# Ends of layers computed in two halves of 256 tokens in a fused four-layer kernel

## What is computed

```python
# layers 0 and 1
h = x * (1 + scale) + shift                  # modulated input of the layer
y = mixer(h)                                 # ends in  mix @ w_out
x = layer_norm(ALPHA * x + (1 + gate) * y, ln_g[l], ln_b[l])
# layers 2 and 3
h = rms_norm(x, norm_g) * (1 + scale) + shift
x = x + gate * (mixer(h) @ w_out)
# end
return rms_norm(x, final_g)
```

## Time and profile before

| | us |
|---|---|
| median of 3 runs | 1336.09 |
| lowest and highest run | 1335.06 and 1337.81 |
| the profiled execution | 1338.26 |
| its span in the profile | 1336.1 |
| PE busy, share of the span | 1300.1, 97% |
| DVE, ACT, POOL busy | 933.7, 573.0, 358.1 |
| mean granted clock of PE, as a share of full speed | 0.992 |

### The profile page before, as it was taken

The page is one execution under the profiler, slowest core; times in us unless marked ns, Lnnn a source line. Parts: engine busy times, 40 slices in busy tenths (PEclk is TensorE's granted clock), DMA queues, the critical chain, the costliest instruction groups (busy, mean ns, idle before and its releaser), DMA issues.

```text
span 1336.1 us, 17324 instructions
## 1 busy us (share of the span) xinstructions
PE 1300.1 (97%) x6589; PEld 1099.5 (82%) x6589; DVE 933.7 (70%) x1347; ACT 573.0 (43%) x863; POOL 358.1 (27%) x257
## 2 busy tenths in 40 slices
PE   6999999999999999999999999999999999999997
PEld 5998888778778888888888788888888788888885
DVE  7765655786667558888678788776784577776663
ACT  1422322221154347666422387653352477634440
POOL 1200200055520004655434122122115322321123
PEclk9999999999989999999999899999999999999998
DMA  9566566456445520111343212214433112211111
GB/s 379 172 207 185 183 201 189 133 154 194 155 119 160 158 87 20 41 52 49 95 141 112 111 64 71 87 48 138 130 99 118 51 64 67 91 64 64 64 63 63
DMA packets 33938, 155.14 MB, mean 116 GB/s; under 512 B 6720, under 2 KB 6848, under 8 KB 22592
## 3 DMA queue, kind: packets, MB, share of 16 engines
q1 hardware_dynamic: 33856, 154.04, 35.9%
HBM read 151.92 MB, written 2.10 MB: 115 GB/s over the span
## 4 chain that ended last, share of the span: by engine, by line
PE 83%; DVE 7%; issue 4%; ACT 3%; POOL 1%; DMA 1%; SPq 0%; DVEq 0%; POOLq 0%; ACTq 0%
PE bank L881 24%; PE bank L883 23%; PE bank L882 23%; PE bank L1204 2%; PE bank L1189 1%; PE bank L1208 1%; PE bank L1049 1%; DVE keep L2272 1%; DVE acc L1769 1%; ACT w_hi L1424 1%; PE bank L888 1%; POOL beta L2395 1%; PE bank L1177 1%; DMA ada_first<-adat 1%; PE bank L1176 1%
## 5 line engine op out<-in xcount | busy, mean ns | idle before, releaser
L881 PE MATMUL bank<-h_lo,w_hi 128*128 128x512 f32 (+1 forms) x1014 | 398.0, 392 | 6.9 <-DVE h_lo L1918 2.5
L883 PE MATMUL bank<-h_hi,w_hi 128*128 128x512 f32 (+1 forms) x1014 | 393.7, 388 | 0.0
L882 PE MATMUL bank<-h_hi,w_lo 128*128 128x512 f32 (+1 forms) x1014 | 393.4, 388 | 0.0
L1727 DVE TENSOR_TENSOR w_lo<-w_raw,w_hi 128x2048 fp32r<-128x2048 f32 (+2 forms) x91 | 206.8, 2272 | 74.6 <-ACT w_hi L1424 74.4
L881 PEld LDWEIGHTS bank<-h_lo,w_hi 128*128 128x128 f32 x1014 | 190.5, 188 | 47.9 <-issue 5.5
L883 PEld LDWEIGHTS bank<-h_hi,w_hi 128*128 128x128 f32 x1014 | 190.3, 188 | 39.6
L882 PEld LDWEIGHTS bank<-h_hi,w_lo 128*128 128x128 f32 x1014 | 190.5, 188 | 38.0 <-issue 0.2
L1424 ACT ACTIVATE w_hi<-w_raw 128x2048 fp32r<-128x2048 f32 (+2 forms) x91 | 166.7, 1832 | 92.9 <-PE bank L883 86.2
L1769 DVE SCALAR_TENSOR_TENSOR acc<-ada_raw,cond_four,acc 128x1024 f32<-128x1024 f32 x62 | 87.9, 1418 | 3.8 <-DMA ada_raw<-adat 0.8
L1506 ACT ACTIVATE tmp<-bank 128x512 f32<-128x512 f32 x48 | 28.8, 600 | 115.6 <-PE bank L883 114.4
L2395 POOL TENSOR_TENSOR beta<-beta,mats 128x256 f32<-128x256 f32 (+1 forms) x40 | 43.8, 1117 | 63.5 <-ACT beta L1686 63.5
(11 more groups left out here) (370 smaller groups left out, 2609.6 us busy)
## 6 DMA issues: line engine op xcount, KB each, us to landing
w_raw<-wt SPq DMA_DIRECT2D x83, 1024.0 KB, 5.4
ada_raw<-adat SPq DMA_DIRECT2D x256, 128.0 KB, 2.9
ada_first<-adat SPq DMA_DIRECT2D x16, 512.0 KB, 12.1
ada_raw<-adat SPq DMA_DIRECT2D x32, 256.0 KB, 5.7
w_raw<-wt SPq DMA_DIRECT2D x8, 640.0 KB, 4.0
spare_raw<-wt SPq DMA_DIRECT2D x3, 1024.0 KB, 7.1
x<-xt SPq DMA_DIRECT2D x4, 512.0 KB, 15.6
out<-outf SPq DMA_DIRECT2D x8, 256.0 KB, 2.2
```

The costliest lines, as they stand in the source:

```text
L881: pe.matmul(dst, ah, bl, start=start, stop=False, skip_group_check=True)
L882: pe.matmul(dst, al, bh, start=False, stop=False, skip_group_check=True)
L883: return pe.matmul(dst, ah, bh, start=False, stop=stop, skip_group_check=True)
L1727: dve.tensor_tensor(w_lo[wb[T]][:, 0:n], w_raw[wb[T]][:, 0:n], f(w_hi[wb[T]][:, 0:n]), ALU.subtract).then_inc(w_lo_done, 1)
```

## The change

A new function `border` writes the steps between two layers. The last chunk (layers 2 and 3: the last two) is computed for tokens 0 to 255 first, then for 256 to 511 in another bank. Between portions of the right half's products stand the left half's sums, its root and its broadcast. Then come the next layer's four chunks for the left half of block 0, the right half's sums, and further items; an item is a block of features for a group of tokens: blocks 0 to 3 left (items 0 to 3), blocks 0 to 3 right (4 to 7), blocks 4 to 7 whole (8 to 11). All dummy matmuls behind the statistics go. Every operation on the way (residual add, square, root, norm, hi, full value, lo, final scaling, output DMA) is done per half for blocks 0 to 3 and the last chunk; POOL's sum for the next to last chunk in layers 2 and 3 is done per half too.

Beside that: the spare tile of each layer is now the first of the two instead of the second, so it is loaded and split one step earlier; one ada piece moves from tile 27's step to tile 31's; the gain sums begin at product 10 of the left half instead of product 8 of the whole; clearing `q_low` moves behind the last item of layer 2; the streams of layer 1 (`x` times `ln_g` plus `ln_b` on ACT) move behind items 8 to 11, two per item.

```diff
--- before.py
+++ after.py
...
+HALF_BLOCKS = 4
+ITEMS = 2 * HALF_BLOCKS + DC - HALF_BLOCKS
...
-    _k = 2 if _T < 28 or 34 <= _T <= 36 or _T in (65, 67, 69) else 1
+    _k = 2 if _T < 27 or _T == 31 or 34 <= _T <= 36 or _T in (65, 67, 69) else 1
...
+    def border(l, last):
+
+        ln, both = l < 3, l == 2
+        parts = {1: (4, 6, 6, 0), 2: (4, 5, 3, 4), 3: (3, 5, 8, 0), 4: (3, 5, 8, 0)}[l]
+        pairs = [(d, k) for d in last for k in range(2 * DC if l < 3 else DC)]
+        at = list(itertools.accumulate(parts))
+
+        def out_half(half, a, b):
+            steps.append(dict(op="out_half", l=l - 1, half=half, pairs=pairs[a:b]))
+
+        def column_sums(half):
+            d = stat(D, 0 if ln else 1, ln, "sums" if ln else "squares", 7, (6, 5) if ln else (6,), half, l)
+            return d, stat(D, 1, False, "derived", 7, (4,), half, l) if both else None
+
+        def blocks(part):
+            steps.append(dict(op="blocks" if l < 4 else "final", l=l, part=part))
+
+        out_half(0, 0, len(pairs))
+        steps.append(dict(op="out_add", l=l - 1, last=last, half=0))
+        out_half(1, 0, at[0])
+        s, rho = column_sums(0)
+        out_half(1, at[0], at[1])
+        steps.append(dict(op="stat_bcast", **s))
+        out_half(1, at[1], at[2])
+        if both:
+            steps.append(dict(op="stat_bcast", **rho))
+            out_half(1, at[2], at[3])
+        left = dict(s=s["stat"], rho=both and rho["stat"])
+        steps.append(dict(op="border_cols", l=l))
+        blocks(0)
+        steps[-1].update(left)
+        steps.append(dict(op="out_add", l=l - 1, last=last, half=1))
+        blocks(1)
+        steps[-1].update(left)
+        if l < 4:
+            steps.append(dict(op="fours", l=l, items=range(1)))
+        s, rho = column_sums(1)
+        right = dict(s=s["stat"], rho=both and rho["stat"])
+        if l < 4:
+            steps.append(dict(op="fours", l=l, items=range(1, 2 if l == 3 else 3)))
+        steps.append(dict(op="stat_bcast", **s))
+        if both:
+            steps.append(dict(op="fours", l=l, items=range(3, 4)))
+            steps.append(dict(op="stat_bcast", **rho))
+        if l < 4:
+            steps.append(dict(op="fours", l=l, items=range({1: 3, 2: 4, 3: 2}[l], ITEMS)))
+        blocks(2)
+        steps[-1].update(right, left_rho=left["rho"])
...
-        chunk("OUT0", T, n=n, l=0, tmp=False)
+        last = chunk("OUT0", T, n=n, l=0, tmp=False, halves=n == DC - 1)
         after_tile(T)
-    s = stat(D, 0, True, "sums", 7, (6, 5))
-    steps.append(dict(op="stat_bcast", **s))
-    steps.append(dict(op="ln", l=1, s=s["stat"]))
+    border(1, [last])
...
-    spare_tiles.append(begin())
+    spare_tiles.append(T)
+    begin()
     for n in range(4):
         chunk("QC", T + n // 2, n=n, sub=n % 2, tmp=False, post=False)
-    T = spare_tiles[-1]
+    T = T + 1
...
-    s = stat(D, 1, False, "squares", 7, (6,))
-    steps.append(dict(op="stat_bcast", **s))
-    steps.append(dict(op="final", s=s["stat"]))
+        border(l + 1, last)
...
         def split_with(T):
 
-            tiles = [T + 1] if T + 1 < NT and T + 1 not in spare_tiles else []
+            if T in spare_tiles:
+                return []
+            if T + 1 in spare_tiles:
+                return [T + 2]
+            tiles = [T + 1] if T + 1 < NT else []
...
+        BLOCK = [(k, tok) for tok in HALVES for k in range(HALF_BLOCKS)] + [(k, ALL) for k in range(HALF_BLOCKS, DC)]
...
-        GAIN_SUMS_AT = 8
+        GAIN_SUMS_AT = 10
...
-            for n in range(DC):
-                sp.wait_ge(fin_done, n + 1)
-                sp.dma_start(out[:, n, :], outf[:, n, :]).then_inc(out_done, 16)
-            sp.wait_ge(out_done, 16 * DC)
+            for half, tok in enumerate(HALVES):
+                for n in range(DC):
+                    sp.wait_ge(fin_done, DC * half + n + 1)
+                    sp.dma_start(out[:, n, tok], outf[:, n, tok]).then_inc(out_done, 16)
+            sp.wait_ge(out_done, 32 * DC)
...
+                rounds = [j for j in items if BLOCK[j][0] < FOUR_ROUNDS]
+                for j in rounds:
+                    k, tok = BLOCK[j]
+                    pe.wait_ge(h_lo_done, H_BASE[l] + j + 1)
+                    for d in order:
+                        bk = CHUNK_BANK[d["C"]]
+                        if j == 0 and bk in banks_right:
+                            pe.wait_ge(post_done, last[-1]["post"])
+                        elif j == 0 and bk in banks_left:
+                            pe.wait_ge(left_done, HALF_COUNT[last[-1]["C"]])
+                        elif j == 0:
+                            wait_taken(pe, BEFORE_IN_BANK[d["C"]])
+                        product(d, k, tok, j == 0, False)
+                if ITEMS - 1 in items:
                     for d in four:
-                        T, a = d["T"], d["sub"] * P
-                        mm3(bank[:, CHUNK_BANK[d["C"]], tok], w_hi[wb[T]][:, a:a + P], w_lo[wb[T]][:, a:a + P],
-                            h_hi[:, 0, tok], h_lo[:, 0, tok], tok is LEFT, False)
-                for c, k in sorted(itertools.product(range(4), range(DC)),
-                                   key=lambda p: (p[1], p[0]) if p[1] < FOUR_ROUNDS else (DC, p[0], p[1])):
-                    d = four[c]
-                    T, a = d["T"], k * HD + d["sub"] * P
-                    if k == 0:
-                        continue
-                    wait_h(layer[0], k)
-                    ins = mm3(bank[:, CHUNK_BANK[d["C"]], :], w_hi[wb[T]][:, a:a + P], w_lo[wb[T]][:, a:a + P],
-                              h_hi[:, k, :], h_lo[:, k, :], False, k == DC - 1)
-                    if k == DC - 1:
+                        for k in range(FOUR_ROUNDS, DC):
+                            pe.wait_ge(h_lo_done, H_BASE[l] + ITEMS - DC + k + 1)
+                            ins = product(d, k, ALL, False, k == DC - 1)
                         ins.then_inc(chunk_full, 1)
+                    h_seen[0] = 8 * l + DC
...
+                    first, final = k == 0, k == len(order) - 1
+                    if first and d["half"] == 0:
+                        wait_taken(pe, BEFORE_IN_BANK[C])
+                    elif first and l < 2:
+                        wait_taken(pe, C - 1)
+                    if l == 1 and d["half"] == 0 and GAIN_SUMS_AT <= k < GAIN_SUMS_AT + 6:
+                        gain_sums((k - GAIN_SUMS_AT) // 2, k % 2)
...
+                    dst = bank[:, (RIGHT_BANK if d["half"] else CHUNK_BANK)[C], tok]
+                    ins = mm3(dst, w_hi[wb[T]][:, a:a + P], w_lo[wb[T]][:, a:a + P], rh[:, f_in, tok],
+                              rl[:, f_in, tok], first, final)
+                    if final:
+                        ins.then_inc(chunk_full if d["half"] else left_full, 1)
...
-                        keep_busy(4 if d["mean"] else 3)
...
+                    if d["half"] == 1:
+                        if d["border"] == 4:
+                            pe.wait_ge(fin_done, DC)
+                        elif d["border"] == 2 and d["lhs"] == "sums":
+                            pe.wait_ge(ln_t, HALF_BLOCKS)
+                        else:
+                            pe.wait_ge(h_t, H_T_BASE[d["border"]] + HALF_BLOCKS)
...
-                        keep_busy(8 if d["stat"] == DERIVED else 4)
...
+            def blocks(d):
+
+                l, part, si, rho = d["l"], d["part"], d["s"], d["rho"]
+                if l == 2 and part == 0:
+                    plain(2, 0, si)
+                    derived_root(rho)
+                    plain(2, 1, si)
+                    scaled(2, 0, rho)
+                    plain(2, 2, si)
+                    low(2, 0)
+                elif l == 2 and part == 1:
+                    scaled(2, 1, rho)
+                    plain(2, 3, si)
+                    low(2, 1)
+                    scaled(2, 2, rho)
+                elif l == 2:
+                    low(2, 2)
+                    scaled(2, 3, d["left_rho"])
+                    plain(2, 4, si)
+                    derived_root(rho)
+                    low(2, 3)
+                    for j in range(5, ITEMS):
+                        plain(2, j, si)
+                        scaled(2, j - 1, rho)
+                        if j >= 6:
+                            low(2, j - 2)
+                    low(2, ITEMS - 2)
+                    scaled(2, ITEMS - 1, rho)
+                    low(2, ITEMS - 1)
+                    dve.memset(f(q_low[64:P, 0, :]), 0.0)
+                    dve.memset(f(q_low[0:64, 1, :]), 0.0)
+                else:
+                    turn = plain if l == 1 else scaled
+                    if part == 0:
+                        turn(l, 0, si)
+                        turn(l, 1, si)
+                        low(l, 0)
+                        turn(l, 2, si)
+                    elif part == 1:
+                        low(l, 1)
+                        turn(l, 3, si)
+                        low(l, 2)
+                    else:
```

(85 more changed lines are left out.)

399 lines of the change are left out of this document (182 added, 217 removed).

## The result

The changed kernel takes 1345.26 us (median of 4 runs, 1344.91 to 1346.02), the kernel before on the same chip 1335.57 us: a ratio of 1.0072, 95% interval 1.006 to 1.0084. It is 9.7 us slower, where 1335.4 was forecast; the time lies outside the range. One execution of one experiment (e5) ran at a granted clock of 0.75 throughout; it is left out, and that kernel was profiled once more as e5b.

The account below looks back on a forecast made before the run. PE's work plus its waits at four layer borders was taken as the bound. Terms -0.5 - 2.9 + 3.0 + 1.1 = 0.7 us gave 1335.4 us against the median of 1336.09; range 1329.5 to 1340.5.

Parts of the forecast that it names:

- the ledger from S to K: Each border, from the layer's last output chunk's first product (layers 2, 3: last two) to next layer's feature block 4's first.
- Border 1, the failed step: End of first layer: second tile's load lands after 5.1 us, PE waits 4.6 to 7.0; border loses 0.5 us.
- Border 1, the clock: At the first layer end, the wait lets the clock fall, costing 2.5 us, bounds 0 and 3.4.
- Border 2: Second layer end: 30.7 us of PE work plus 11.8 of waits, K - S 42.4 against 39.53, a loss of 2.9.
- Rival C: Slower: waits at border 2's items 2 to 4 let the clock fall, first spare takes 7.5 us; 1339.4 us, chance 0.20.
- Border 3: Third layer end: no gain sums or second root, K - S 25.7 against 28.67 us, a gain of 3.0.
- Border 4: Last layer end to output DMAs: left outputs leave beside the right half's matmuls, a gain of 1.1 us.
- The price of a split product: PE's products cut into halves: 0.013 us more each by the rows, 3.8 us for 300 more product instructions.
- the lower price set beside it: Trainium skill's fixed 2.5 ns per warm matmul: all splits cost 0.75 us, and the sum would be 3 us lower.
- the likeliest case: Whole kernel: borders 3 and 4 win what 1 and 2 lose, 0.7 us in sum, 1335.4 us; chance 0.45.
- Rival B: Faster: first spare lands after 5.1 us, clock holds at border 1, which gives 3.2; whole 4.4, 1331.7 us, chance 0.28.

Follow-up runs that it names:

- e5: Changed kernel, with SP waiting until the second tile's load at border 1 has landed before issuing later loads: ratio 1.0066.
- e5b: The kernel of e5 once more, for a profile at the usual clock: 1347.51 us in one run.
- e11: Changed kernel, with the position DMA at border 1 issued two tile loads later: 1343.86 us, ratio 1.0069.
- e1: Changed kernel, with the second tile's load at border 1 issued right behind the spare's, ahead of the next ada piece and position DMA: 1337.09 us, ratio 1.0008.
- e3: Changed kernel, with 44 dummy matmuls ahead of PE's sum that waits for the left add at border 1: 1342.94 us, ratio 1.0065.
- e6: Changed kernel, with the early second load of e1 and the moved gain sums of e4 together: 1332.73 us, ratio 0.9973.
- e10: e6 with dummy matmuls, one ada piece moved, and at border 2 DVE's split of item 2 ahead of the right half's statistics: 1328.37 us, ratio 0.9950.
- e4: Changed kernel, with border 2's twelve gain sums between the first right-hand products instead of within the left half: 1343.10 us, ratio 1.0056.
- e7: e1 with border 2's gain sums spread in pairs and the left half's column sums one product later: 1330.63 us, ratio 0.9964.

## Why the prediction was wrong, step by step

- **What bounds the kernel, the ledger from S to K, and that the rest is alike:** right. The untouched stretches differ by 0.0 to 0.4 us.
- **Border 1, the failed step:** "Landing 5.1, ACT 1.9, DVE 2.3, one piece 1.3: DVE comes to the left half's add at S + 12.2 to 14.6". Order and issue time were right; the landing was taken from one row, of a load behind which nothing was issued for 6.5 us, for a load that the same text put right behind a position DMA and ahead of further loads. It measured 10.9 in the changed kernel's profile, and 9.2 and 8.0 in two more executions of the same order of DMAs; what makes it long stays open, since e5b and e11 come out within that spread or at its edge. The wait was therefore 10.2 instead of 4.6 to 7.0. That this landing holds DVE, and DVE holds PE, is shown by e1, where the load is early and the border 10.3 us shorter. The bounds widened the spare's landing (5.1 or 7.5) but not this one.
- **Border 1, the clock:** that the wait lets it fall was right, the price too small: 2.5 forecast, bounds 0 and 3.4, 3.3 to 3.6 measured (e3). The rest, 27.5 of work and about 2 of waits, is e6's 29.42.
- **Border 2:** the steps were right; what the sum left out was a fall of the clock. With the clock held it takes 41.62 (e3) against 42.4 forecast: gain wait 1.63 for 2.0, second root 0.35 for 0.8, item 2 1.40 for 1.8, item 3 1.15 for 1.5, first right block 1.97 for 2.2, three later blocks 1.7 for 2.4, first h_lo 0.60 for 0.7. These are idle times from the end of the last matmul; start to start each costs some 0.25 us more (item 2 in the changed kernel: 766.33 - 764.66 = 1.67, and the next matmul 0.22 behind instead of 0.12), so that 41.62 less the 30.7 of work leaves 10.9 for the 11.8 of the sum. That item 2 waits because of its place in DVE's queue is e10's result. What wasn't in the sum is the clock's fall at the gain sums: 3.1 us in the changed kernel's profile; 6.8 to 6.9 in four others, their second fall at the items included. Rival C had a fall at this border, but at items 2 to 4 and from waits; in four profiles of this code it does fall there too, for 3.4 us, but not in the changed kernel's, so C as stated isn't what made it slow. The rule that C named, of the Trainium skill, "TensorE: Matmul & The Clock Gate", "HAM oscillation — how this bites in real kernels", speaks of waits between bursts; the items show such falls, while e4's fall stands in a stretch of PE work without any wait.
- **Border 3:** right, 26.12 for 25.7; its only wait is GpSimd's, 0.21 for 0.3. **Border 4:** right, 0.99 for 1.1.
- **The price of a split product**, 0.013 from the rows: right. In the changed kernel's timeline products of 256 columns start 0.12 apart, and border 1 in e6 and border 3 come out at the sum or a little above it, not below, as the lower price set beside it would have them.
- **Numbers:** the likeliest case was wrong and the outcome lay past the range, since the two errors, the landing (10.2 of wait for 5.8) and the clock (about 1 more at border 1, 3.1 at border 2, there less 0.8 that the waits fell short of the sum), went the same way. Rival B's border 1, a gain of 3.2 where DVE isn't late, is what e1 makes true by moving one DMA (31.77 for 36.26); faster as a whole the kernel is only with the gain sums changed too, in e6 and e7.

## What to carry to other kernels

A load's landing time belongs to its place in the queue (4.8 to 6.5 us for the spare tile's near 342 and 8.0 to 10.9 for the second tile's near 355, over the profiles of the changed kernel, e3, e4, e5b and e11): before taking it from a row, look at whether as much is issued right ahead of it and behind it, and give it bounds. One execution isn't enough to price what stands around it: the same order of DMAs gave 8.0, 9.2 and 10.9 us here. When a layer end is cut finer so that PE has less to wait in, check what stands in DVE's queue ahead of the first short step; here one load issued 13 us earlier was worth 8 to 10 us, and turned the loss at its border into a gain. Give a stretch of many one-column matmuls bounds with and without a low clock, even where PE doesn't wait, and compare mean clocks before comparing single runs.

## What the runs showed of the hardware that was not expected

- The granted clock fell to 1.2 GHz within a stretch in which PE was never idle (e4, S + 9.6), behind twelve one-column sums among 256-column products. In the same code at the same place it fell for 0, 6.8 or 17 us in different executions, which, with the 3.4 us at the items that went with the 17, moved the border by up to 6.9 us.
- A busy DMA engine doesn't say how much it moves: over 356 to 359 us of the changed kernel, with the position broadcast, ada pieces and tile loads under way, the engines were busy for 0.85 to 0.99 of the time and moved 76 to 186 GB/s; over 359 to 361 us of e11 they moved 393 to 410 at 0.96 to 1.01.
- One 1 MB load, with the same DMAs issued ahead of it and behind it, landed after 8.0, 9.2 and 10.9 us in three executions (e3, e4, the changed kernel).
- Two 1 MB loads issued 0.4 us apart, with little beside them (e1, from 341.7 on), landed after 6.0 and 8.0 us, both by 350.1: early enough for ACT to find the second in place at 353.
